# The retention scores of layer 1 as two products of 64 rows in place of one product with a zero-padded operand

## What is computed

```
def retention_scan(q, k, v, log_gamma, s0):
    ...
    def step(s, qkv):
        qc, kc, vc = qkv
        scores = jnp.einsum('bhid,bhjd->bhij', qc, kc) * intra
        o = (jnp.einsum('bhij,bhjv->bhiv', scores, vc)
             + jnp.einsum('bhid,bhdv->bhiv', qc * q_dec[..., None], s))
        s = s * c_dec[..., None] + jnp.einsum('bhjd,bhjv->bhdv', kc * k_dec[..., None], vc)
        return s, o
```

## Time and profile before

| | |
|---|---|
| median of 3 runs | 2929.33 us |
| profiled execution, span | 2929.5 us |
| PE busy | 2734.4 us (93%) |
| DVE busy | 1951.2 us (67%) |
| ACT busy | 713.3 us (24%) |
| POOL busy | 1065.4 us (36%) |
| mean granted clock of PE | 0.964 |
| first stage of layer 1 with scores | about 1776 to 2051 us |

### The profile page before, as it was taken

One profiled execution on the slowest core, in us unless ns is written; L12 is line 12 of the kernel. 1 busy time (PEld: TensorE's weight loads), 2 busy tenths in 40 slices (PEclk: granted clock), 3 DMA queues, 4 the chain that ended last, 5 costly groups with the idle time before them and its releaser, 6 DMA issues.

```text
span 2929.5 us, 36939 instructions
## 1 busy us (share of the span) xinstructions
PE 2734.4 (93%) x13212; PEld 2227.6 (76%) x13212; DVE 1951.2 (67%) x3295; ACT 713.3 (24%) x1454; POOL 1065.4 (36%) x973
## 2 busy tenths in 40 slices
PE   6999998797999999999999699998788999999996
PEld 4777776576888888888887478886677888888885
DVE  4789973856676677677668789863865454454456
ACT  3233324433111111110111323333523111111111
POOL 1344353664111111111112645563763332323325
PEclk9999998798999999999999799998899999999998
DMA  8322322531122222222220212211521111111111
GB/s 240 96 90 68 107 78 74 160 92 44 58 74 70 79 79 72 72 72 72 72 42 24 90 58 63 61 50 53 152 67 50 51 50 44 56 43 50 50 43 65
DMA packets 246651, 214.60 MB, mean 73 GB/s; under 512 B 60384, under 2 KB 203280, under 8 KB 246544
## 3 DMA queue, kind: packets, MB, share of 16 engines
q1 hardware_dynamic: 149488, 120.94, 13.9%
q10 hardware_dynamic: 97056, 92.29, 10.4%
HBM read 190.56 MB, written 22.63 MB: 73 GB/s over the span
## 4 chain that ended last, share of the span: by engine, by line
PE 80%; DVE 10%; POOL 4%; DMA 2%; issue 2%; ACT 1%; SPq 1%; ACTq 0%; POOLq 0%; DVEq 0%
PE bank L571 15%; PE bank L573 14%; PE bank L572 14%; PE bank L1071 9%; PE bank L1072 9%; PE bank L1073 9%; PE bank L651 1%; DVE work L1625 1%; PE bank L979 1%; PE bank L1004 1%; DVE bank L1675 1%; PE bank L1003 1%; PE bank L938 1%; PE bank L939 1%; PE bank L940 1%
## 5 line engine op out<-in xcount | busy, mean ns | idle before, releaser
L1500 POOL TENSOR_TENSOR w_lo<-raw,w_hi 128x1024 fp32r<-128x1024 f32 x120 | 288.1, 2402 | 1119.9 <-ACT w_hi L1334 1119.9
L1071 PE MATMUL bank<-x_hl,w_hi 128*128 128x512 f32 (+1 forms) x1280 | 476.3, 372 | 0.2 <-ACT work L1322 0.2
L1770 DVE TENSOR_TENSOR work<-work 128x512 f32<-128x512 f32 (+1 forms) x160 | 156.9, 980 | 476.0 <-ACT work L1322 476.0
L1072 PE MATMUL bank<-x_hl,w_hi 128*128 128x512 f32 (+1 forms) x1280 | 473.6, 370 | 0.0
L1073 PE MATMUL bank<-x_hl,w_lo 128*128 128x512 f32 (+1 forms) x1280 | 473.0, 370 | 0.0
L1794 DVE TENSOR_TENSOR work<-work,bank 128x512 f32<-128x512 f32 x576 | 390.0, 686 | 122.4 <-PE bank L573 111.5
L571 PE MATMUL bank<-w_hi,h_hi 128*128 128x512 f32 x1152 | 450.5, 391 | 7.2 <-DVE work L1794 5.3
L572 PE MATMUL bank<-w_lo,h_hi 128*128 128x512 f32 x1152 | 449.0, 390 | 0.0
L573 PE MATMUL bank<-w_hi,h_lo 128*128 128x512 f32 x1152 | 448.9, 390 | 0.0
L1675 DVE SCALAR_TENSOR_TENSOR bank<-work,bank 128x512 f32<-128x512 f32 (+1 forms) x580 | 407.2, 702 | 18.9
L1334 ACT ACTIVATE w_hi<-raw 128x1024 fp32r<-128x1024 f32 x120 | 126.8, 1059 | 783.3 <-PE bank L573 585.6
(11 more groups left out here) (141 smaller groups left out, 4412.2 us busy)
## 6 DMA issues: line engine op xcount, KB each, us to landing
raw<-in_w_ff ACTq DMA_DIRECT2D x128, 512.0 KB
work<-in_w_ada SPq DMA_DIRECT2D x48, 512.0 KB
plain_words<-in_w_ada ACTq DMA_DIRECT2D x64, 256.0 KB
raw<-in_w_in SPq DMA_DIRECT2D x60, 256.0 KB
plain_words<-in_w_ada SPq DMA_DIRECT2D x16, 512.0 KB, 12.1
raw<-in_w_out SPq DMA_DIRECT2D x10, 512.0 KB
gate_rows<-work SPq DMA_DIRECT2D x72, 64.0 KB, 1.6
retention_rows<-work SPq DMA_DIRECT2D x72, 64.0 KB, 1.6
```

The lines of the kernel that those rows point to most:

```text
L1071: nc.tensor.matmul(o, slot(mlp_slot(l, f), 0)[:, wc], x_hi[:, k, cols], start=k == 0, stop=False)
L1072: nc.tensor.matmul(o, slot(mlp_slot(l, f), 0)[:, wc], x_lo[:, k, cols], start=False, stop=False)
L1500: nc.gpsimd.tensor_tensor(slot(mlp_slot(l, sl), 1), raw[:, un % 2, :], slot(mlp_slot(l, sl), 0).bitcast(F32), ALU.subtract).then_inc(w_rea ...
L1770: nc.vector.tensor_tensor(a32, a32, a32, ALU.mult).then_inc(S["h_sq"], 1)
```

## The change

In layer 1 the scores of a pair are two products. Each takes the 64 partitions of its head: stationary operand `qk_t[r64, t, 1, :]` (128 columns), moving operand `qk_t[r64, t, 0, :]` (128 columns). The first writes the first 128 columns of one bank, the second those of the bank after it. ACT's two copies into `q_diag` and the count `qd_done` are gone in layer 1; PE waits for `post_evac` in place of `qd_done`. DVE's product with the mask reads both banks in one instruction.

Scores that are not late use banks 5 and 6, and values go to bank 7 in layer 1. Late scores use banks 0 and 1 for even r and 5 and 6 for odd r. The first late score (r = 25) waits for `prob_done` of r = 24 and no longer for that of r = 23. Layer 0 is as it was.

```diff
+    counts["qd_done"] = 0 if l else ret_steps
...
-        banks = [es.enter_context(nc.psum_tensor(f"bank{i}", [P, 512], F32)) for i in range(8)]
+        all_banks = es.enter_context(nc.psum_tensor("bank", [P, 8, 512], F32))
+        banks = [all_banks[:, i, :] for i in range(8)]
...
-        def ps_values(r, late):
-            return banks[2 + r % 2] if late else banks[6]
+        def ps_head_scores(r, late):
+
+            first = (0, 5)[r % 2] if late else 5
+            return all_banks[:, first:first + 2, 0:P]
+
+        def ps_values(l, r, late):
+            return banks[2 + r % 2] if late else banks[7 if l else 6]
...
+                first_late = min(row_of(l, a[1], a[2]) for a in plan if a[0] == "scores" and a[3])
...
+                    elif a[0] == "scores" and l:
+                        _, p, t, late = a
+                        r = row_of(l, p, t)
+                        pe.wait_ge(S["post_evac"], s0["post_evac"] + r + 1)
+                        if late:
+                            pe.wait_ge(S["evac_q"], s0["evac_q"] + n * PAIRS)
+                        if late and r > first_late:
+                            pe.wait_ge(S["prob_done"], s0["prob_done"] + r - 1)
+                        elif r:
+                            pe.wait_ge(S["prob_done"], s0["prob_done"] + r)
+                        for h in range(2):
+                            r64 = slice(h * DK, (h + 1) * DK)
+                            mm = nc.tensor.matmul(ps_head_scores(r, late)[:, h, :], qk_t[r64, t, 1, :], qk_t[r64, t, 0, :], start=True, stop=True)
+                        mm.then_inc(S["score_done"], 1)
...
-                    elif a[0] == "scores":
+                    elif a[0] == "scores" and not l:
                         _, p, t, late = a
                         r = row_of(l, p, t)
                         if r >= 2:
...
-                        nc.vector.tensor_tensor(probs[:, r % 2, :], ps_scores(r, late), masks[:, 2 * p:2 * p + 2, :].rearrange("p a b -> p (a b)"), ALU.mult).then_inc(S["prob_done"], 1)
+                        if l:
+                            nc.vector.tensor_tensor(probs[:, r % 2, :].rearrange("p (h i) -> p h i", h=2), ps_head_scores(r, late),
+                                                    masks[:, 2 * p:2 * p + 2, :], ALU.mult).then_inc(S["prob_done"], 1)
```

More of the change, by code:

```diff
@@ L276, in layer_counts @@
         counts[name] = q_tiles
-    for name in "evac_q qd_done sd_done score_done prob_done val_done comb_a comb_b comb_done".split():
+    for name in "evac_q sd_done score_done prob_done val_done comb_a comb_b comb_done".split():
         counts[name] = ret_steps
@@ L994, in _ @@
                         pe.wait_ge(S["sd_done"], s0["sd_done"] + r + 1)
-                        ps_o = ps_values(r, late)
+                        ps_o = ps_values(l, r, late)
                         if late:
@@ L1632, in _ @@
                             dve.wait_ge(S["val_done"], s0["val_done"] + r - 1)
-                        nc.vector.tensor_tensor(probs[:, r % 2, :], ps_scores(r, late), masks[:, 2 * p:2 * p + 2, :].rearrange("p a b -> p (a b)"), ALU.mult).then_inc(S["prob_done"], 1)
+                        if l:
+                            nc.vector.tensor_tensor(probs[:, r % 2, :].rearrange("p (h i) -> p h i", h=2), ps_head_scores(r, late),
+                                                    masks[:, 2 * p:2 * p + 2, :], ALU.mult).then_inc(S["prob_done"], 1)
+                        else:
+                            nc.vector.tensor_tensor(probs[:, r % 2, :], ps_scores(r, late), masks[:, 2 * p:2 * p + 2, :].rearrange("p a b -> p (a b)"), ALU.mult).then_inc(S["prob_done"], 1)
                     elif a[0] == "values":
```

## The result

The changed kernel takes 2935.14 us (median of 21 runs), the kernel before, run beside it, 2930.82 us: ratio 1.0015, 95% interval 1.0009 to 1.0021, or +4.4 us with 2.6 to 6.2. The forecast was +5.05 us on 2929.33, that is 2934.4. The change is slower, by less than the 0.2% (5.9 us) that was named as what can be told from no change, and by 0.65 us less than forecast. (As a time, 2935.14 is 0.7 us over 2934.4, since the kernel before now has 2930.82 in place of 2929.33.) The profiled executions have spans of 2931.0 us (after) and 2929.5 us (before). These single executions differ by only 1.5 us: the one of after comes to the stage 1.7 us earlier (its values product that answers to the first of the earlier trace rows starts 1.68 us before it), loses 3.95 us in the stage, and gains about 0.8 us again behind it.

What follows compares the result with a forecast made beforehand. TensorE was taken as the bound, busy 93% of the span and carrying 80% of the chain that ended last. Projection stretch 3.8 plus tail 1.25 gave +5.05 us on 2929.33, so 2934.4 us, range 2924.0 to 2938.5.

Steps and rivals of the forecast that it cites:

- The price of a visit: On TensorE, each score's way into and out of the divided array: 0.62 us against 0.43, +0.19 us per score.
- Rival B: On TensorE, division by rows empties nothing and both heads run at once: 0.21 us per score, 2924.3 us; chance 0.25.
- How many scores pay: Projection stretch: 20 of 24 scores pay 0.19 us, four hidden where values wait for DVE: +3.8 us.
- The new wait: Tail: second score of the last pair waits for prob_done of the first, sharing banks 5 and 6: values +0.75 us.
- The tail: After the projection stretch: new wait 0.75 plus two dearer scores 0.5, later scores in the stores' shadow: +1.25 us.
- The parts at no price: ScalarE's 64 dropped copies, values in bank 7 and DVE's reading of two banks: 0 us.
- A: On TensorE, the two heads' four loads run in a row and set the pace: 0.81 us per score, 2939.5 us; chance 0.25.
- C: On TensorE, no emptying, but heads run in turn or loads fill the gain: score 0.43 us, 2929.8 us; chance 0.17.
- the likeliest of four: On TensorE, scores divided, array emptied, loads overlapping: 2934.4 us, own range 2931.5 to 2937.5; chance 0.33.

Runs made afterwards that it cites:

- e4: Changed kernel with both products of a score in the same row group (head 0 twice, head 1 left out): 2943.04 us, one execution.
- e8: Changed kernel with each head's score product made twice within one stay in the divided array: 2944.01 us, one execution.
- e1: Changed kernel with scores as two products of all 128 rows from the padded operand, ScalarE's copies back, same banks and waits: 2929.89 us, ratio 0.9997 to before.
- e2: Changed kernel with the first score of the last pair (r = 24) in banks 0 and 1, so r = 25 doesn't wait: 2934.97 us, ratio 1.0018 to before.
- e5: Changed kernel with only the 8 tail scores (r = 24 to 31) undivided again: 2933.58 us, ratio 1.0013 to before.
- e6: Changed kernel with only the 24 scores of the projection stretch undivided again, the tail's 8 still divided: 2931.73 us, ratio 1.0008 to before.
- e3: Changed kernel with the queries-by-states product also divided, beside the next tile's score in one visit; r = 24 in banks 0 and 1: 2927.09 us, ratio 0.9990 to before.
- e7: The kernel of e3 measured again, for its interval against before: 2927.10 us, ratio 0.9992 to before.

## Why the prediction was right, point by point

**The price of a visit: right.** +0.19 was forecast and +0.19 is in the step (1.58 to 1.77), 0.62 us for the score as written. How it is composed fits as well: the two heads at once with their loads (e4, e8), and a cost of going in and out that is the same with one pair of heads inside and with two (after, e8). The forecast's terms lie in the step where they should: 0.09 ahead of the score; 0.10 + 0.21 + 0.11 = 0.42 from the score to the next product, measured 0.43; and 0.11 for a load that nothing covers, measured +0.10 behind the key-value product, whose loads begin with it (1811.29) where they began 0.21 us ahead of it before (1812.36). The single records of the trace show the parts within the 0.43 too: in e4 the second record of the score starts 0.21 us after the first and the others 0.11 after one another, so that a first load of 0.10 stands uncovered, and the next ordinary load starts 0.20 us after the last record, 0.11 of it its stream and 0.1 emptying. e1 adds that 0.02 of the 0.19 would be there without any row group. What the forecast took as one price has two values, 0.19 and, ahead of the turning L986, 0.15.

The Trainium skill, "TensorEngine Tiling (Array Packing)", Key Properties, says that changing the tiling mode drains TensorE. The trace agrees, and gives the price for row groups, 0.41 us in and out, or 0.39 without the 0.02 that e1 shows for the greater number of records. The rule behind Rival B, from the Trainium skill's "TensorE: Matmul & The Clock Gate", Part 3 (products in separate row groups begin a few ns apart), agrees with after and e8 too, where the records of the two heads start 6 to 7 ns apart; in e4, in one row group, they don't. It says nothing of the way in and out, and that decided.

**How many scores pay: about right, their price a little too high.** 20 x 0.19 = 3.8 us were forecast; the stretch V0 to V23 is 2.53 us longer than before, and 3.05 longer than in e1. Between V8 and V15 and again between V16 and V23 it is +1.21 each, 0.173 for each of seven scores; 20 of them would be 3.5 us. Between V0 and V7 it is +0.81, and between V7 and V8 -0.15, since a part went into the waits, which are 0.37, 0.37 and 0.33 shorter, as said. Between V15 and V16 before has 43.78 us, after 43.23. There before has 0.47 us of idle time ahead of its key-value product (L979, 1960.14) that neither after nor e1 has, though e8 has one of 1.78 us; this looks like a trait of the single execution, not of the change, but isn't shown to be. So the term was 0.7 us too high (3.8 against 3.05) to 1.3 (against 2.53).

**The new wait: right in its place, too high in size.** 0.75 was forecast; it is 0.44 (12.39 to 12.83), and 0.43 disappears in e2. The time at which the second score can start was nearly right (0.56 us behind the start of DVE's product at 2030.60; forecast 0.49). What was mis-sized is the divided score at half clock: 1.1 us was taken, and it is 0.73 from its start to the values (2031.16 to 2031.89). With undivided products, in e1, the same wait costs 0.71.

**The tail: near in sum, by errors that cancel.** Forecast +1.25, measured +1.42, of which the wait is 0.44 and what follows V24 0.98, where 0.5 was forecast. A tile takes 2.73 us where it took 2.56, +0.17, and 0.25 was forecast. So what a visit loses is the same in ns at the lower clock, 0.17 to 0.19, though the columns take twice as long. A pair of heads takes 0.43 us there (from the score to the values 0.73 us in after, 1.16 in e8), against 0.85 for the undivided score, a saving of 0.42. So going in and out costs 0.59 us and not 0.82: it doesn't double with the halved clock.

The step that was sized too low is the path behind the wait. The forecast let two scores count, ahead of the row sum of the third tile (r = 26), and put all others in the shadow of SP's queue and of the stores. The chain that ended last shows where the tail leaves PE, in before and then in after:

```profile
2041.20 0.30 DVE work L1652
...
2043.41 0.43 SPq L795
...
2043.88 5.63 DMA retention_rows<-work
```

```profile
2043.94 0.97 PE bank L1026 x2
...
2045.77 0.30 DVE work L1678
...
2046.09 5.69 DMA retention_rows<-work
```

In before it leaves with the sum of the fourth tile (r = 27, 2041.20), runs through four loads that SP issues, and the store of r = 28 goes out at 2043.88, 13.28 us after V24. Three scores lie on that way, not two: from V24 to the sum of r = 27 it is 10.60 us in before and 11.15 in after, +0.55. In after the chain stays on PE for one tile more, to the sum of r = 28, and the store goes out at 2046.09, 14.20 us after V24. SP had issued its last load by 2045.67 (begun at 2045.24, 0.43 us), so PE makes the store 0.4 us later than SP would. A clock risen as in before would have spared that (an estimate); that it stays at half, below, was not foreseen. The landing, 5.69 against 5.63, makes 0.06. Together +0.98. DVE's last wait for a store is 0.67 us, after 2.62 and 1.75: little of the shadow is left.

```profile
2051.87 0.29 DVE L1678 TENSOR_TENSOR work<-bank,work 128x128 f32<-128x128 f32 x1 [0.67 <-DMA retention_rows<-work]
```

**The parts at no price: right.** DVE reads two banks in the time of one: the products with the mask L1656 take 411, 415 and 425 ns (lowest, median, highest of 32), practically the same as 412, 415 and 425 of L1633 in before (72, both layers). ScalarE's copies gave nothing: after has none of them and no step that is shorter for it, and where the first score of the tail no longer waits for them (it starts at 2025.91, right behind the key-value product), what follows waits for DVE all the same. That ScalarE is busy for about a third of the stretches is so in the projection stretch; in the tail it was half, 8.20 of 16 us, which changes nothing here.

**The rivals.** A falls by e4 and e8, C by the same, B by the step of after. The forecast was the likeliest of four at a chance of 0.33; what made it so, one visit of L651 in layer 0, held: a division by columns that costs 0.31 us to go in and out told the price of one by rows, with the exposed first load of 0.10, to within 0.01 us. That one case by columns would carry over so exactly to rows was not known, and is in part luck. So is the total, +5.05 against +4.4: the terms that were too high (0.7 to 1.3 in the stretch, 0.3 in the wait) and the one that was too low (the tail behind the wait, 0.5) partly cancel.

## What to carry to other kernels

Products of 64 rows per head, each head in its own row group, run at once, but each visit to the divided array between ordinary products costs about 0.4 us here (0.6 at half clock). Weigh that against the stream it saves, here 0.22 us for a score. One divided product to a visit lost here; two in one visit came out a little ahead. Look for a visit of any divided product in the trace of the kernel that you have: here one of another shape gave the price of the way in and out before anything was built. Taking copies off an engine that nobody waits for was no gain, and a second bank per buffer brought a wait where two uses had stood side by side.

## What the runs showed of the hardware that was not expected

**The clock in the tail.** PE's granted clock after 2038 us, in before and then in after (columns as in the table by stretch):

```profile
2038.00:2042.00 4.00, 4.00 (x19) 3.42 (x18) 2.76 (x11) 2.58 (x9) 0.00 (x0) 0.72 0.39 110
2042.00:2046.00 4.00, 2.39 (x15) 1.75 (x14) 1.79 (x8) 0.98 (x4) 0.00 (x0) 1.00 0.93 239
```

```profile
2038.00:2042.00 4.00, 4.00 (x15) 2.56 (x14) 1.59 (x6) 0.62 (x2) 0.00 (x0) 0.50 0.11 33
2042.00:2046.00 4.00, 4.00 (x17) 2.81 (x17) 2.39 (x10) 1.23 (x4) 0.00 (x0) 0.50 0.92 245
```

In before the clock rises soon after 2040 us and is at 1.00, the 2.4 GHz level, from 2042 to 2046; a tile then takes 1.31 to 1.37 us. In after it stays at 0.50, the 1.2 GHz level, to the stage's end, though PE shows no gap there either: 4.00 of 4.00 us busy. The experiments side with the division: e1 and e5, with undivided scores in the tail, have the rise, and e6, e3, e2, e4, e7 and e8, with divided ones, don't, e8 with twice the products in each visit. Counting before and after, that is three executions with the rise and seven without (e3 and e7 are one kernel). First e1 and then e6 in the same stretch:

```profile
2038.00:2042.00 4.00, 4.00 (x31) 3.69 (x29) 3.53 (x14) 2.61 (x9) 0.00 (x0) 1.00 0.67 179
```

```profile
2038.00:2042.00 4.00, 4.00 (x16) 2.46 (x15) 1.77 (x7) 0.95 (x4) 0.00 (x0) 0.50 0.11 33
```

It costs little here, some 0.4 us of the tail by the estimate above. With the fast clock PE only waits longer for the stores: in e5 the clock has risen and then

```profile
2050.44 1.11 PE L1029 MATMUL bank<-work 128*128 128x64 f32 x4 [3.92 <-DVE work L1662]
```

PE stands 3.92 us. Why the clock stays low isn't settled. The records of the divided products or the time in which the array empties could each be it, and no run here takes them apart. That less time goes to loads can't be the whole of it: from 2034 to 2038 us, with both clocks at 0.50, loads take 2.90 us in after and 3.37 in before, but in e3 they take 3.41, more than in before, and its clock doesn't rise either. In a tail that isn't hidden by stores the lost clock would cost over 1 us per tile (an estimate: 2.73 us against 1.37 and the 0.19 of a visit), far more than the visit itself. Layer 0's scores are undivided in all runs, so whether the same would happen there isn't known.

**Loads in row groups.** The four loads of a score in two row groups lie in 0.30 us in after; in one row group they take 0.52 (e4), and eight in two row groups 0.53 (e8). So the loads of two row groups hide each other as the products do. Ahead of the visit they hide behind nothing: in all three kernels the first load begins with the score itself, after 0.33 us without a load.
